# The queue that issues 30 small parameter loads: SyncE's, or GpSimd's in front of its share of the first norm

## The reference

```
x = x + 0.5 * swiglu(rms_norm(x, ff1_norm), ff1_w_gate, ff1_w_up, ff1_w_down)     # 1024 -> 2816 -> 1024
h = rms_norm(x, mix_norm);  q, k, v, u = split(h @ w_in)
attn = banded attention with sinks and ALiBi(q, k, v, sink)
ssm  = S5 state space(u; a_re, a_im, b_re, b_im, c_re, c_im, d_skip, log_dt), then gelu and a GLU (w_glu, b_glu)
x = x + concat(rms_norm(attn, attn_out_norm), rms_norm(ssm, ssm_out_norm)) @ w_out
x = x + 0.5 * swiglu(rms_norm(x, ff2_norm), ff2_w_gate, ff2_w_up, ff2_w_down)
out = rms_norm(x, final_norm)
```

## Time and profile before

| | |
|---|---|
| Time, median of 3 runs (lowest to highest) | 1892.21 us (1892.01 to 1893.86) |
| Profiled execution, first to last instruction (span) | 1891.5 us |
| PE busy; PEld; DVE; ACT; POOL | 96%; 79%; 40%; 24%; 23% of the span |
| Mean granted TensorE clock | 0.976 |
| q1 (SP's transfers) | 107.35 MB, 20.8% of the 16 engines' span |
| q0 (GpSimd's transfers) | 4.42 MB, 0.6% |

### The profile page before, as it was taken

How to read it: one execution, slowest core, us unless ns; L and a number is a source line. 1 busy time by engine, 2 the same in 40 slices (tenths; PEclk the granted TensorE clock), 3 DMA queues, 4 the chain that set the end, 5 groups by cost and what they waited for, 6 DMA issues and landing times.

```text
span 1891.5 us, 22799 instructions
## 1 busy us (share of the span) xinstructions
PE 1820.5 (96%) x8284; PEld 1493.1 (79%) x8284; DVE 761.9 (40%) x1067; ACT 455.6 (24%) x745; POOL 431.8 (23%) x894
## 2 busy tenths in 40 slices
PE   6899999999999999999798799999999999999998
PEld 5788888888888887788576687888888888888886
DVE  5243243334323434612864545334324333432345
ACT  6211211111111113423447434111121111111113
POOL 2588776750000002400333333000000000000003
PEclk8999999999999999899888899999999999999999
DMA  5311212121121111123922031111111111112102
GB/s 129 85 45 45 78 59 74 55 77 45 33 67 44 44 44 45 62 78 76 120 67 67 12 112 56 56 45 55 33 55 55 44 44 55 44 35 65 44 33 89
DMA packets 166442, 112.33 MB, mean 59 GB/s; under 512 B 32576, under 2 KB 156096, under 8 KB 166144
## 3 DMA queue, kind: packets, MB, share of 16 engines
q1 hardware_dynamic: 165120, 107.35, 20.8%
q0 software_dynamic: 1280, 4.42, 0.6%
HBM read 98.68 MB, written 13.07 MB: 59 GB/s over the span
## 4 chain that ended last, share of the span: by engine, by line
PE 88%; ACT 3%; SPq 3%; DVE 2%; DMA 2%; POOL 1%; issue 1%; DVEq 0%; ACTq 0%; POOLq 0%
PE bank L646 28%; PE bank L647 28%; PE bank L648 28%; POOL ssq L1689 1%; SPq L543 1%; PE bank L882 1%; PE bank L883 1%; DMA Mt<-k_scratch 1%; ACT sco L1234 0%; PE bank L884 0%; DVE htmp L1366 0%; ACT hT_hi L1056 0%; PE bank L841 0%; PE bank L661 0%; SPq L535 0%
## 5 line engine op out<-in xcount | busy, mean ns | idle before, releaser
L646 PE MATMUL bank<-hT_hi,w_lo 128*128 128x512 f32 x1728 | 685.3, 397 | 17.4 <-DVE hT_lo L1379 6.2
L647 PE MATMUL bank<-hT_lo,w_hi 128*128 128x512 f32 x1728 | 679.2, 393 | 0.0
L648 PE MATMUL bank<-hT_hi,w_hi 128*128 128x512 f32 x1728 | 678.9, 393 | 0.0
L646 PEld LDWEIGHTS bank<-hT_hi,w_lo 128*128 128x128 f32 x1728 | 328.7, 190 | 92.1 <-issue 14.7
L1332 DVE TENSOR_TENSOR w_lo<-raw,w_hi 128x1024 fp32r<-128x1024 f32 x157 | 193.0, 1240 | 480.8 <-ACT w_hi L1026 480.8
L647 PEld LDWEIGHTS bank<-hT_lo,w_hi 128*128 128x128 f32 x1728 | 328.9, 190 | 69.9 <-issue 1.9
L648 PEld LDWEIGHTS bank<-hT_hi,w_hi 128*128 128x128 f32 x1728 | 328.4, 190 | 69.4
L1689 POOL TENSOR_TENSOR ssq<-ssq,sqt 128x512 f32<-128x512 f32 x54 | 78.1, 1447 | 1106.5 <-ACT sqt L1040 1102.6
L1416 DVE SCALAR_TENSOR_TENSOR xT<-bank,xT 128x512 f32<-128x512 f32 x352 | 241.0, 690 | 188.0 <-PE bank L648 187.9
L646 PE MATMUL bank<-aT_hi,w_lo 128*128 128x512 f32 x704 | 275.1, 391 | 4.0 <-DVE aT_lo L1409 3.1
L648 PE MATMUL bank<-aT_hi,w_hi 128*128 128x512 f32 x704 | 273.9, 389 | 0.0
(11 more groups left out here) (168 smaller groups left out, 980.2 us busy)
## 6 DMA issues: line engine op xcount, KB each, us to landing
raw<-in_ff_w_gate_dram SPq DMA_DIRECT2D x44, 512.0 KB, 3.7
raw<-in_ff_w_up_dram SPq DMA_DIRECT2D x44, 512.0 KB, 3.7
raw<-in_ff_w_down_dram SPq DMA_DIRECT2D x44, 512.0 KB, 3.3
x_in<-in_x_dram SPq DMA_DIRECT2D x8, 512.0 KB, 6.2
out_dram<-osb SPq DMA_DIRECT2D x8, 512.0 KB, 2.7
raw<-in_w_out_dram SPq DMA_DIRECT2D x26, 128.0 KB, 2.9
raw<-in_w_out_dram SPq DMA_DIRECT2D x13, 256.0 KB, 3.3
raw<-in_w_in_dram SPq DMA_DIRECT2D x6, 512.0 KB, 4.2
```

The lines of the kernel that those rows point to most:

```text
L646: nc.tensor.matmul(o, wl, rh, start=first, stop=False)
L647: nc.tensor.matmul(o, wh, rl, start=False, stop=False)
L648: return nc.tensor.matmul(o, wh, rh, start=False, stop=last)
```

## The change

The body of `small_loads` moves from SP's program to GpSimd's. It is split in two: 26 transfers are issued behind the four stores of zeros and in front of `norm(N_FF1)`; the four loads of c (`c_loads`) follow `norm(N_FF1)`, behind a wait for x_squared >= 8 (all eight squares of x done). Their sizes, sources, destinations and semaphores stay as they were. SP's `among` keeps only `load_x(1)`, so that unit 3 follows unit 2 directly.

```diff
@@ SP
         def among(n):
             if n == 0:
                 load_x(1)
-            elif n == 2:
-                small_loads()
@@ POOL
+        def small_loads():
+            for col, g, kt in ((8, mix_norm[0], 8), (20, ssm_out_norm[0], 4),
+                               (24, ff2_norm[0], 8), (32, final_norm, 8)):
+                pool.dma_start(gains[:, col:col + kt], g.rearrange("(k p) -> p k", p=P)).then_inc(consts_loaded, 16)
+            for kv in range(NKV):
+                pool.dma_start(gains[kv * HD:(kv + 1) * HD, 16:20],
+                              attn_out_norm[0][kv * 256:(kv + 1) * 256].rearrange("(g d) -> d g", d=HD)
+                              ).then_inc(consts_loaded, 16)
+            pool.dma_start(bglu[:, :], b_glu[0].rearrange("(k p) -> p k", p=P)).then_inc(consts_loaded, 16)
+            for g2 in range(2):
+                for nn in range(2):
+
+                    for kv in range(NKV):
+                        src = sink[0].rearrange("(v a g) -> g v a", v=2, g=2)[g2, kv].partition_broadcast(HD)
+                        pool.dma_start(sinkt[g2 * HD:(g2 + 1) * HD, kv, nn, :], src).then_inc(consts_loaded, 16)
+            pool.dma_start(dsk[:, :], d_skip[0].rearrange("(g h) -> h g", h=GH)).then_inc(consts_loaded, 16)
+            for n, a in enumerate((a_re, a_im)):
+                for g2 in range(2):
+                    pool.dma_start(par[g2 * NS:(g2 + 1) * NS, n, :],
+                                  a[0].rearrange("(j g) p -> g p j", g=2)[g2]).then_inc(params_loaded, 16)
+            for g2 in range(2):
+                pool.dma_start(par[g2 * NS:(g2 + 1) * NS, 2, :],
+                              log_dt[0].rearrange("(j g) -> g j", g=2)[g2].partition_broadcast(NS)
+                              ).then_inc(params_loaded, 16)
+            for n, b in enumerate((b_re, b_im)):
+                for g2 in range(2):
+                    pool.dma_start(b_raw[g2 * NS:(g2 + 1) * NS, n, :, :],
+                                  b[0].rearrange("(j g) p h -> g p j h", g=2)[g2]).then_inc(params_loaded, 16)
+
+        def c_loads():
+            pool.wait_ge(x_squared, KD)
+            for n, c in enumerate((c_re, c_im)):
+                for a in range(2):
+                    pool.dma_start(c_in[:, n, :, a, :],
+                                  c[0].rearrange("(i g) h p -> (g h) i p", g=8)).then_inc(c_loaded, 16)
...
             pool.dma_start(zv[n][:, 0:(T - 1) * GH], zero[:, :]).then_inc(zero_stored, 16)
+        small_loads()
         norm(N_FF1)
+        c_loads()
```

More of the change, by code:

```diff
@@ L515, in load_x @@
                 sp.dma_start(x_in[h][:, t % 4, :], x[0, t * P:(t + 1) * P, :]).then_inc(x_loaded[t], 16)
[L517 to L548, removed]
         def among(n):
```

## The result

The kernel after takes 1914.76 us (median of 4 runs, 1914.11 to 1915.77) against 1893.03 us for the kernel before (4 runs): ratio 1.0115, 95% interval 1.0101 to 1.0129, or 21.7 us more. The profiled execution has a span of 1914.3 us where it was 1891.5. It is slower, as forecast, and inside the range, but by twice the forecast 11 us.

The account below looks back on a forecast made before the run. PE, busy 96%, bounds the kernel. Issues of 33 us delay the low parts by 18.4 us; less 7.3 saved gives +11.1, a 1902.6 us span, 1903.3 us measured; forecast's own range 1896 to 1915, widened to 1885 to 1918.

Parts of the forecast that it names:

- what the old place costs: PE's waits for c and unit 3's w_lo, 4.87 us, plus 2.39 us at the low clock: 7.3 us given back.
- delay minus 7.3: Net change: delay of GpSimd's first low part, none made up later, less 7.3 us saved; zero gain at 21.9 us of issues.
- the price of an issue: GpSimd's time for the 26 small loads: 14.0 us low, 28.9 by the line, 40.6 high.
- line through GpSimd's two stores: From stores of 128 and 256 pieces: 0.402 us each issue plus 1.125 ns each piece, 28.9 us for 26.
- the case that I called a tie: Rival 2: the 26 issues take 18.1 to 25.7 us, net within 3.8 us, about 1892 us; chance 0.13.
- the hold by the broadcast loads: SP's b issue took 11.51 us behind broadcast loads; if the transfer's shape causes it, GpSimd is held up too.
- X: Time of GpSimd's 26 issues in front of its low parts, taken as 33 us.
- the share of 0.05: DMA share during SP's long b issue, read as about one engine of 16 serving the broadcast loads.
- The step that failed: Small pieces joining the full DMA engines in the first 20 us can delay x and unit 1, at no added cost.
- d: Delay of GpSimd's first low part, X - 14.6 us where positive; forecast 18.4 us.
- the prediction's account: Whole kernel: net change is d - 7.3 us, since PE is the bound from there to the end.
- its doubt about a spread over 16: The skill would spread a load of slowest dimension 64 over 16 engines; the prediction said the 0.05 share disagrees.

Follow-up runs that it names:

- The version between the halves: Kernel before, ten broadcast loads kept on SP behind unit 2, GpSimd's other 16 issues between its low parts of the first and second x half: 1886.79 us.
- the three kernels whose first matmul was late without re-reading on GpSimd's queue: After with broadcasts back on SP, 1889.99 us; after with no re-reading at all, 1892.20; before with 24 memsets delaying GpSimd's low parts, 1895.37.
- all 26 issues between the halves: Kernel after, its 26 GpSimd issues, re-reading ones included, moved between the low parts of the first and second half: 1894.07 us, ratio 1.0000.
- the ten loads alone: Kernel before, only the eight sink and two log_dt loads issued by GpSimd in front of the low parts, 20 staying on SP: 1905.91 us.
- log_dt without re-reading: Kernel after, the two log_dt loads reading a_re at different addresses, same count of pieces, sinks still re-reading: 1897.55 us, ratio 1.0030.

## Why the prediction was wrong

- **Right: what the old place costs.** 4.87 us of waits and 2.4 us of clock, 7.3 in all. The version between the halves gains 7.2, and the three kernels whose first matmul was late without re-reading on GpSimd's queue fit delay minus 7.3: -4.6 against -4.0, -2.8 against -2.8, +2.3 against +1.5. That the first two fit to a few tenths is luck. In their traces TensorE loses another 3.0 and 1.2 us on the way to the seventh half unit: it waits 2.95 and 2.44 us in front of the last transposes of x, where it waited 1.41 before, and the granted clock behind it is 0.50 and 0.54 (39.2 to 42.5 us) where it was 1.00.
- **Wrong in size: the price of an issue.** The line through GpSimd's two stores gave 1.125 ns for a piece and 28.9 us for the 26; without re-reading they took 19.0. From 128 to 1024 pieces an issue grows by about 0.3 us, or 0.3 ns for each piece. The line went through two points that differed in more than the count (another tensor, other sizes, an address from a register), and its slope is four times too steep; which of these made the second point dear was not tested. 19.0 us is the case that I called a tie.
- **Right by half: the hold by the broadcast loads.** It was named, with the earlier trace rows, as what would add to the line. It is real (5.47 us of X = 24.5, not 33), and its cause is the re-reading: without it both GpSimd's gap and SP's 11.5 us vanish. That the loads sit on one engine of 16, as the prediction read the share of 0.05, does not hold; more on this below. X was still 8.5 us too high, which by itself would have made the forecast +11.1 into +2.6.
- **The step that failed**: "This can hold back x and unit 1, but they are needed from 26 us on plus d, so it hides under d." Unit 1 took 35.31 us and came at 50.43; needed were 26 + 9.9. I had seen that the re-reading loads keep SP's own queue from draining for some 20 us and priced it only as a hold of the issuing queue, not as a hold of everything else on the same DMA engines. At the first matmul the delay was 9.9 us, at the first half unit of the second gate it was 25.6 (59.99 against 34.42): 15.7 us more. With the log_dt pair free of re-reading those are 8.6 and 10.9 (45.29), 2.2 us more. So 13.4 of the 15.7 us are the pair's, with 1.3 at the first matmul; the whole time says 16.1 (21.8 - 5.7).
- **The same step, seen at unit 1.** It took 8.1 us to land before, 17.3 with GpSimd's small loads but no re-reading, 20.9 with the sinks re-reading, and 35.3 with log_dt as well. Against the time at which it was needed (26 plus the delay of the first matmul) it came at 30.4 for 30.5, at 36.6 for 34.6 and at 50.4 for 35.9: "it hides" holds for the small pieces, and fails by 2 and by 14.5 us for the re-reading.

The steps from before to after: issues in front of the low parts, with the wait for unit 3 saved, -2.8 us; re-reading of the sinks +8.5; of log_dt +16.1; each uncertain by some 3 us or more. They add up to the whole because each is the difference to the next kernel, so the sum is no check of its own. With the true X and nothing held, the prediction's account gives +2.6 us, which it called a tie. The forecast had the right sign by luck, through two errors that partly cancelled.

The Trainium skill, "DMA: Bandwidth & Descriptors", section "Queues, rings and completion order", says that each DMA engine takes turns between its queues but drains a whole packet, of up to 64 descriptors, before it switches. The traces agree on the packets: SP's small loads show as 17797 packets under 512 bytes, about one for each piece, while in the first 60 us after, the DMA view gives 960 packets for all of GpSimd's 16384 pieces and its stores. The packet records in the traces (start, duration, bytes) say how long one lasts. With all 26 issues between the halves, 32 packets of 256 bytes, which is 64 pieces of 4 bytes and makes up the 2048 pieces of log_dt, last 2.4 to 8.4 us each, up to 16 of them at a time, from 44.5 to 62.9 us. Without re-reading, GpSimd's packets of 256 bytes last 0.13 us in the mean. So long packets, and as many at once as there are engines, are shown. The records do not name the engine, so that SP's transfers stood behind them on the same engines is the likely reading and not shown.

The records also settle what the share of 0.05 on SP's queue meant. From 38 to 51 us before, while log_dt is read, the DMA view gives this:

```profile
DMA packets 1397, 0.01 MB, mean 0 GB/s; under 512 B 1397, under 2 KB 1397, under 8 KB 1397
```

That is 107 pieces per us, with a record of 7 ns for each: the share is small because the records are short, and says nothing about the number of engines. The prediction's reading of it as one engine, and its doubt about a spread over 16, rested on that. On GpSimd's queue the 2048 pieces took 17.7 us after, 18.4 with all issues between the halves and 20.0 with the ten loads alone, which is 102 to 116 per us. So log_dt is read at about the same rate on both queues, though up to 16 long packets are under way at once on GpSimd's.

Open: why the rate is so low. That the pieces lie close together is not enough. GpSimd's packets of the sink loads begin from 12.4 to 23.7 us where they re-read (log_dt without re-reading), and from 12.4 to 18.4 us where each load reads 128 neighbouring numbers, 512 bytes in all.

## What to carry to other kernels

When a transfer moves to another queue, look up how long it takes to land where it stands now, not only how long it takes to issue: two loads that landed after 16 us for 4 KB held up x and a weight unit once they shared the DMA engines with them, so keep such a load away from transfers that the first matmuls wait for. A broadcast from HBM over partitions was such a load here; from different addresses, the same count of pieces landed in a third of the time. And before an idle gap of one engine is filled, look for a second gap: GpSimd had one of 17 us between the halves, where 16 of the issues cost nothing.

## What the runs showed of the hardware

- A load that reads 16 numbers for each of 64 partitions by broadcast, 1024 pieces of 4 bytes, lands after 16.3 us on SP's queue; the loads of a_re in its place, as many pieces, land after 5.1 us (median of the four in that kernel).
- Re-read pieces of 4 bytes move at 107 per us on SP's queue (38 to 51 us before) and at 102 to 116 per us on GpSimd's (log_dt in three kernels). On GpSimd's queue 64 of them make one packet, of 2.4 to 8.4 us with all issues between the halves.
- Issued by GpSimd, two such loads made a difference of 16 us in the whole kernel; SP's four x issues took 25.84 us, and 4.62 before, with ten re-reading loads (eight sinks, two log_dt) on GpSimd's queue.
- Small pieces alone delay a weight load too: unit 1 took 17.3 us to land beside GpSimd's 26 loads without re-reading, 8.1 us before.
- GpSimd's issue time depends little on the pieces: 0.59 us for 128, 0.67 to 0.77 for 512, 0.83 to 0.92 for 1024.
- GpSimd can be held inside a sequence of issues (5.47, 4.17 and, between the halves, 0.86 us with re-reading loads on the way, none without).
